# Output projection of a two-layer encoder step: two token tiles taken block by block instead of tile by tile

## The reference, cut to what matters

```
h = rms_norm(x);  o = attention(h, cache)            # layer 0: differential, layer 1: forgetting
x = x + o @ w_out                                    # w_out is 1024 x 1024
h2 = rms_norm(x)
x = x + experts(h2)    # 16 experts: gate and up 1024 x 512, down 512 x 1024, top 2 in one group of 4
```

## Time and profile before

| | |
|---|---|
| median of 3 runs | 989.9 us (987.43 to 990.96) |
| the profiled execution | 985.11 us |
| its span in the trace | 983.3 us |
| TensorE busy | 923.4 us, 94% of the span |
| granted TensorE clock, mean | 0.984 of full speed |
| DMA, mean over the span | 276 GB/s, 271.60 MB moved |

### The profile page before, as it was taken

How to read it: one execution, slowest core, us unless ns; L and a number is a source line. 1 busy time by engine, 2 the same in 40 slices (tenths; PEclk the granted TensorE clock), 3 DMA queues, 4 the chain that set the end, 5 groups by cost and what they waited for, 6 DMA issues and landing times.

```text
span 983.3 us, 11921 instructions
## 1 busy us (share of the span) xinstructions
PE 923.4 (94%) x4642; PEld 572.8 (58%) x4642; DVE 408.0 (41%) x867; ACT 308.3 (31%) x608; POOL 157.1 (16%) x218
## 2 busy tenths in 40 slices
PE   3999989799999999999899999989899999999997
PEld 3777766688544444443477777766787444443443
DVE  4666367524212323223738544344435122322223
ACT  4554477513111111112434444444323111111110
POOL 5214322301000000000321254442010000000000
PEclk9999999799999999999999999999899999999999
DMA  9743731239699999999524463442768999999995
GB/s 286 286 129 128 246 107 55 105 125 391 242 420 425 423 424 423 426 410 426 177 90 129 136 180 118 132 131 82 301 231 329 366 420 426 421 427 423 425 425 205
DMA packets 56778, 271.60 MB, mean 276 GB/s; under 512 B 5824, under 2 KB 6064, under 8 KB 32144
## 3 DMA queue, kind: packets, MB, share of 16 engines
q1 hardware_dynamic: 47824, 242.64, 62.3%
q0 software_dynamic: 8896, 28.16, 9.2%
HBM read 261.01 MB, written 9.77 MB: 275 GB/s over the span
## 4 chain that ended last, share of the span: by engine, by line
PE 83%; DMA 6%; DVE 5%; ACT 3%; issue 1%; POOL 1%; SPq 0%; DVEq 0%; ACTq 0%
PE ps L1449 20%; PE ps L1467 11%; PE ps L1046 7%; PE ps L1047 7%; PE ps L1048 7%; DMA w_raw<-in_moe_w_up 3%; PE ps L1099 2%; PE ps L1100 2%; PE ps L1480 2%; PE ps L1481 2%; PE ps L1259 2%; PE ps L1424 2%; PE ps L1255 2%; PE ps L1054 2%; PE ps L1409 1%
## 5 line engine op out<-in xcount | busy, mean ns | idle before, releaser
L1449 PE MATMUL ps<-w_raw,xT 128*64 128x512 f32 x368 | 159.1, 594 | 0.0
L1449 PE MATMUL ps<-w_extra,xT 128*64 128x512 f32 x456 | 142.2, 594 | 4.0 <-DMA w_extra<-in_moe_w_up 2.3
L1571 DVE TENSOR_TENSOR w_lo<-w_raw,w_hi 128x2048 fp32r<-128x2048 f32 x36 | 82.1, 2288 | 45.2 <-ACT w_hi L739 45.2
L1046 PE MATMUL ps<-w_hi,hT_hi 128*128 128x512 f32 x224 | 93.6, 418 | 4.2 <-DVE w_lo L1571 3.1
L1449 PEld LDWEIGHTS ps<-w_extra,xT 128*64 128x64 f32 x456 | 43.9, 137 | 86.8 <-issue 86.8
L1048 PE MATMUL ps<-w_hi,hT_lo 128*128 128x512 f32 x224 | 89.7, 400 | 0.0
L1047 PE MATMUL ps<-w_lo,hT_hi 128*128 128x512 f32 x224 | 89.5, 400 | 0.0
L1449 PE MATMUL ps<-w_more,xT 128*64 128x512 f32 x200 | 85.1, 593 | 0.0
L739 ACT ACTIVATE w_hi<-w_raw 128x2048 fp32r<-128x2048 f32 x36 | 68.5, 1910 | 39.4 <-PE ps L1100 36.5
L1467 PE MATMUL ps<-w_raw,hidT 128*64 128x512 f32 x176 | 75.5, 596 | 0.1
L1467 PE MATMUL ps<-w_extra,hidT 128*64 128x512 f32 x224 | 68.3, 597 | 0.0
(11 more groups left out here) (290 smaller groups left out, 1634.9 us busy)
## 6 DMA issues: line engine op xcount, KB each, us to landing
w_extra<-in_moe_w_up SPq DMA_DIRECT2D x32, 1024.0 KB, 14.7
w_extra<-in_moe_w_down SPq DMA_DIRECT2D x28, 1024.0 KB, 16.3
w_extra<-in_moe_w_gate SPq DMA_DIRECT2D x25, 1024.0 KB, 15.1
w_raw<-in_moe_w_gate SPq DMA_DIRECT2D x24, 1024.0 KB, 15.5
w_raw<-in_moe_w_down SPq DMA_DIRECT2D x22, 1024.0 KB, 16.1
w_raw<-in_moe_w_up SPq DMA_DIRECT2D x22, 1024.0 KB, 13.6
w_raw<-in_fox_w_in SPq DMA_DIRECT2D x16, 1024.0 KB, 5.5
w_more<-in_moe_w_gate SPq DMA_DIRECT2D x15, 1024.0 KB, 19.9
```

Of the source, the lines that this page charges most:

```text
L1046: mm(out, a_hi, b_hi, start=start, stop=False)
L1449: ins = mm(ps[j * CAP:(j + 1) * CAP, bank, :], xT[:, i % 2, kb, j * CAP:(j + 1) * CAP], buffer(U.slot)[:, k * F:(k + 1) * F], start=(kb == ...
L1571: v.tensor_tensor(w_lo[:, U.slot, :], w_raw[:, U.slot, :], w_hi[:, U.hslot, :].bitcast(F32), ALU.subtract).then_inc(lo_ready, 1)
```

## The change

Tile 0 still goes through both column blocks. Then tile 1 and tile 2 go through column block 0, and after that both go through column block 1. The function takes the blocks as an argument, and tile 1 raises `out_done` only after its second block.

```diff
-                def out_tile(t):
+                def out_tile(t, blocks=range(OUT_BLOCKS)):
 
                     ts = slice(t * P, (t + 1) * P)
-                    for b in range(OUT_BLOCKS):
+                    for b in blocks:
                         out = ps[:, 2 * t + b, :]
...
-                    if t < 2:
+                    if t < 2 and b == OUT_BLOCKS - 1:
                         ins.then_inc(L["out_done"], 1)
...
                 out_tile(0)
                 transposes(B, o, o_ready, "o_tr", counts=last_items, tiles=(2,))
-                out_tile(1)
-                out_tile(2)
+                for b in range(OUT_BLOCKS):
+                    out_tile(1, (b,))
+                    out_tile(2, (b,))
                 transposes(B, h2, "h_ready1", "tr1", tiles=(0, 1), spread=True)
```

## The result

The changed kernel takes 999.98 us (median of 4 runs, 997.57 to 1002.81), the one before 990.36 us (median of 4, 987.43 to 990.96). The ratio is 1.0107, with a 95% interval of 1.007 to 1.0145. The change made the kernel 9.6 us slower. I had forecast 994.9 us, +5.0, with 998.2 as the upper end: the sign was right, the size about half.

A forecast was written before the change was run, and what follows sets the result against it. TensorE, busy 94% of the span, was taken as the bound. Late stores 0.8 (layer 0) and 3.2 (layer 1) plus clock 1.0 gave +5.0 us on the 989.9 median: 994.9 us, range 990.3 to 998.2.

The forecast's parts named there:

- Where tile 1 and the units move: Output projection on TensorE: tile 1 finishes 3.75 us later; out units 0 and 1 are over 5.6 us earlier.
- The early units bring nothing: Expert weight loads: four of eight issued 5.6 us earlier, put at 0 because nobody waits for those bytes.
- Tile 2's 0.9 us are hidden: Tile 2's sum behind tile 1's norm on VectorE: 0.9 us late per layer, covered before TensorE's transposes, cost 0.
- Late stores, "+0.8" and "+3.2": Second h2 store 3.75 us later delays VectorE's low parts and routing: +0.8 us in layer 0, +3.2 in layer 1.
- slack of 2.98 us: VectorE's idle time before the first routing instruction in layer 0, expected to swallow most of the 3.75 us delay.
- The clock, "between 0 and 1.7 I take +1.0 us": TensorE stands still 3.8 us before layer 1's ranks; a likely fall to half clock costs 0 to 1.7, taken +1.0 us.
- More falls: Rival: clock falls in layer 0 too, or over two stretches, each up to 1.7 us more: 996.5 to 998; chance 0.10.
- Partly hidden: Rival: h2 stores land 1.5 to 2 us sooner than assumed as weights thin out: 991 to 992.5 us; chance 0.17.
- the stores don't matter: Rival: h2 stores land in something like 3.2 us and slack takes all: 989.9 us, no change; chance 0.12.
- the early loads pay: Rival: weight stream bounds the experts, so the early loads remove the 2.3 and 1.2 us waits: 986.4 us; chance 0.05.

The follow-up runs named there:

- e2: Changed kernel with the eight expert loads held until both stores of h2 have landed: 990.2 us, ratio 1.0003.
- e5: Changed kernel with its four early loads held until out unit 2 is over, tile 1 still late: 997.9 us, ratio 1.0074.
- e9: Changed kernel with expert loads held until both h2 stores land and 3 instead of 6 fillers behind tile 0's logits: 987.4 us, ratio 0.9966.
- e4: Kernel before with 2 instead of 10 filler matmuls ahead of the wait for `selected`: 993.6 us, ratio 1.0046.
- e1: Changed kernel with 18 instead of 10 filler matmuls ahead of the wait for `selected`: 996.3 us, ratio 1.0051.
- e10: The kernel of e7 measured once more, on the chip of e9: 984.8 us, ratio 0.9945.
- e3: Changed kernel with GpSimd storing tile 0 of h2 before the root of tile 1: 994.3 us, ratio 1.0053.
- e7: Kernel before with expert loads held until both h2 stores land and 3 instead of 6 fillers between logits of tiles 0 and 1: 988.6 us, ratio 0.9951.

## Why the prediction was right or wrong

**Where tile 1 and the units move: right.** 3.75 us later and 5.6 us earlier, to the row.

**The early units bring nothing: right.** The waits for weights in the experts are 1.8 and 1.2 us after the change, where they were 2.3 and 1.2, and the median of e2, which issued the loads 8 to 16 us later than the change (counted from the end of the projection), is the one of before. I had not seen that the early loads can do harm: in the traces they lengthen the stores by 0.5 to 1.3 us in layer 0 (e5).

**Tile 2's 0.9 us are hidden: right.** In the after trace the sum of tile 2 starts when the norm of tile 1 ends. e2 is at the level of before, and in e9, with three fillers fewer, 0.2 us of it show.

**Late stores, "+0.8" and "+3.2": right in kind, 1.4 us short.** Measured +2.00 and +3.46. The latency was 12.2 us where I had used 10.9 and 11.8, and e2 shows that it hangs on the weights: 2.9 us without them. (The 3.2 us of the earlier trace rows, which I took for stores with no weights beside them, are not quite that: from 116 to 120 us, where the two stores went out, the queue of the weights moved 0.39 MB.) In layer 0 more than half of the slack of 2.98 us that I counted on was there only because the fillers before it happened to run at half clock in the profiled execution. After the change they ran at full clock. Against e4, a kernel without the late tile in whose trace they ran at full clock too, the routing of layer 0 is 15.97 - 12.28 = 3.7 us late, not 2.0. A slack that rests on such a stretch is not one to subtract from.

**The clock, "between 0 and 1.7 I take +1.0 us": this step failed.** Its size in the traces is +5.9 us: 3.26 us in layer 0 and 2.67 in layer 1. In the medians e1 takes 3.7 us away and e4 adds 3.4. Three things were wrong with it. First, I gave it to layer 1 only. But TensorE waits for routing in both layers. By my own terms the pause of layer 0 would have been 0.6 + 0.8 = 1.4 us. It was 4.29: about 0.6 as before, 2.0 of late routing, and 1.7 because the earlier fillers ran at full clock and TensorE stood at the wait that much sooner. Second, I took the price from the fall in the earlier trace rows, where twelve filler halves lost 1.7 us. What stands behind this pause is the ranks, six filler halves (2.91 instead of 1.54 us) and the wide matmuls of the gather, eight of the twelve at half clock, all on the path; a fall there costs what that work costs again. Third, I took 1.7 us as the most that one fall can cost. The half clock lasted from 248.9 to beyond 255 us. e1 and e4 tie the cost to the pause from both sides: fill it and the step from `sel` to `x_slots` is at 5.63 us, open it in the kernel before and it is at 8.2 to 9.0.

So the sum is 2.0 + 3.5 + 3.3 + 2.7 = 11.4 us in the profiled executions, of which 9.6 us show in the medians. The first two terms are what I had as 4.0. The Trainium skill's rule that an idle engine drops to 1.2 GHz (TensorE: Matmul & The Clock Gate, Part 1), which I had named as pointing to the upper end, agrees with these traces as far as the pauses ahead of the ranks go: the six of 3.0 to 4.3 us and the one of 1.5 us were followed by half clock, the one of 1.0 us and those of 0.6 us were not. It doesn't account for every fall: in layer 0 of the kernel before and of e10 the clock fell after 0.53 us of idle time.

**The rivals.** "More falls" came closest, with a chance of 0.10 and a price that was too small for the same reason. "Partly hidden", "the stores don't matter" and "the early loads pay" did not occur. I gave them 0.34 together.

**Still open.** The 2 us of the span outside the changed stage: no run told whether they belong to the change or to scatter. And e3's median lies 3 us above what its trace would give. No run told either what makes the clock fall in some executions among the narrow matmuls and not in others.

## What to carry to other kernels

When a late event makes an engine wait, price two things: the wait, and the work behind it at the clock that the wait leaves. Here the second was as large as the first. Filler matmuls held the clock here where they left a pause of 1.0 us or less, and not where they left 1.5 us or more; a change that moves the end of the wait must move the fillers too. And small stores that release a buffer should not be issued into a stream of large loads that nobody needs yet: holding the loads back cut their latency from 12 to 3 us, at a cost that no median shows. All the stores have to be out first: the third one went out beside the held loads and took 10 us.

## What the runs showed of the hardware

- A 512 KB store to HBM landed in 2.9 us with the load queue empty (e2). With eight loads of 1 MB in flight, the second of two such stores was over 10.9 to 12.2 us after its issue (before, after, e1, e4, e5). With the first one sent 14 us ahead of it, it was 8.96 and 9.66 us (e3).
- TensorE stood still ahead of the ranks for 0 to 0.6, 1.0, 1.5, 3.0 to 3.8 and 4.1 to 4.3 us in different kernels. The ranks and the gather ran at full clock behind the first two, and all or part of them at half clock behind all others.
- Between narrow matmuls (128x20) the same code has executions with and without a fall of the clock: the second logits took 1.86 us in e7 and 3.44 us in e10, and the first fillers of layer 0 4.52 us before and 2.84 us in e4.
